# Stick-breaking attention: query blocks of a head in reverse order

## The reference

```python
def stick_breaking_attention(q, k, v):          # 8 heads of 64
    qh = heads(q) * (Dh ** -0.5)
    for blk in range(seq // SB_BLOCK):          # 8 query blocks of 128
        start, end = blk * SB_BLOCK, (blk + 1) * SB_BLOCK
        logits = jnp.einsum('bhtd,bhsd->bhts', qh[:, :, start:end], kh[:, :, :end])
        causal = jnp.arange(end)[None, :] < (start + jnp.arange(SB_BLOCK))[:, None]
        log_remain = jnp.where(causal, jax.nn.log_sigmoid(-logits), 0.0)
        log_after = lax.cumsum(log_remain, axis=3, reverse=True) - log_remain
        weights = jnp.where(causal, jnp.exp(jax.nn.log_sigmoid(logits) + log_after), 0.0)
        outs.append(jnp.einsum('bhts,bhsd->bhtd', weights, vh[:, :, :end]))
```

## Time and profile before

| | us |
|---|---|
| median of 3 runs | 1866.09 (1864.34 to 1867.01) |
| profiled execution | 1864.38, its span 1862.6 |
| TensorE busy, of the span | 1555.1 (83%) |
| VectorE, ScalarE, GpSimd busy | 527.9, 385.5, 265.1 |
| mean granted TensorE clock | 0.924 |
| the mixers stage | 439.7 to 880.1 |
| TensorE in heads 0 to 7, start to start | 54.75, 56.07, 56.51, 55.98, 54.03, 53.01, 56.93, 53.08 |

### The profile page before, as it was taken

One profiled execution on the slowest core, in us unless ns is written; L12 is line 12 of the kernel. 1 busy time (PEld: TensorE's weight loads), 2 busy tenths in 40 slices (PEclk: granted clock), 3 DMA queues, 4 the chain that ended last, 5 costly groups with the idle time before them and its releaser, 6 DMA issues. The chain is left out here.

```text
span 1862.6 us, 19239 instructions
## 1 busy us (share of the span) xinstructions
PE 1555.1 (83%) x6818; PEld 872.1 (47%) x6818; DVE 527.9 (28%) x678; ACT 385.5 (21%) x682; POOL 265.1 (14%) x386
## 2 busy tenths in 40 slices
PE   7999999996989988898389937777778777866997
PEld 4558644444777777776144533232223232323443
DVE  4220133202444444444223241111111111112323
ACT  2221221112343343333021100000000001022221
POOL 1000002101222222221112011111111111110110
PEclk9999999998999999999699958898899898987999
DMA  5220246303110111100711125999999999972220
GB/s 173 72 68 30 81 143 144 96 11 77 29 29 0 28 28 28 28 0 19 304 68 74 39 102 195 419 397 401 399 401 398 402 395 395 408 295 110 94 89 34
DMA packets 93347, 302.95 MB, mean 163 GB/s; under 512 B 13808, under 2 KB 48000, under 8 KB 67328
## 3 DMA queue, kind: packets, MB, share of 16 engines
q1 hardware_dynamic: 83808, 285.69, 41.0%
q0 software_dynamic: 9504, 16.80, 2.4%
HBM read 281.42 MB, written 38.85 MB: 172 GB/s over the span
## 5 line engine op out<-in xcount | busy, mean ns | idle before, releaser
L1381 PE MATMUL pe_gu<-w_gu,xT 128*64 128x512 f32 x1024 | 272.6, 694 | 107.7 <-DMA w_gu<-in_w_expert_up 104.2
L209 PE MATMUL ps<-hT,w_ct 128*128 128x512 f32 x640 | 278.6, 596 | 3.4 <-DVE hT L347 3.4
L1381 PEld LDWEIGHTS pe_gu<-w_gu,xT 128*64 128x64 f32 x1024 | 83.7, 158 | 274.7 <-issue 273.0
L209 PEld LDWEIGHTS ps<-hT,w_ct 128*128 128x128 f32 x640 | 121.4, 191 | 152.7 <-issue 151.2
L724 DVE TENSOR_TENSOR_SCAN Pm<-rem,Pm 128x128 f32<-128x128 f32 (+3 forms) x96 | 97.5, 1016 | 178.2 <-ACT brk L665 178.2
L799 POOL TENSOR_TENSOR wt<-brk,Pm 128x128 f32<-128x128 f32 (+3 forms) x96 | 83.0, 864 | 340.1 <-DVE Pm L724 340.1
L1049 PE MATMUL p_x<-w_o,mT 128*128 128x512 f32 x256 | 121.4, 630 | 2.4 <-DVE mx L1004 1.3
L1474 DVE TENSOR_TENSOR hs<-sg,pe_gu 128x256 f32<-128x256 f32 x32 | 13.5, 421 | 379.9 <-ACT sg L1445 379.9
L1399 PE MATMUL pe_y<-w_d,hTe 128*64 128x512 f32 x512 | 115.5, 592 | 1.1 <-DVE ys L1479 1.1
L1702 PE MATMUL f_pg<-w_gu,f_xT 128*128 128x512 f32 x256 | 114.7, 602 | 1.1 <-ACT f_xT L1620 1.1
L223 PE MATMUL psk<-w_tok,hT 128*128 128x260 f32 (+1 forms) x384 | 111.7, 453 | 0.0
(11 more groups left out here) (266 smaller groups left out, 1738.7 us busy)
## 6 DMA issues: line engine op xcount, KB each, us to landing
w_gu<-in_w_expert_gate SPq DMA_DIRECT2D x64, 1024.0 KB, 13.7
w_gu<-in_w_expert_up SPq DMA_DIRECT2D x64, 1024.0 KB, 15.8
w_d<-in_w_expert_down SPq DMA_DIRECT2D x64, 1024.0 KB, 8.9
w_ct<-in_w_in SPq DMA_DIRECT2D x20, 512.0 KB, 4.4
y_sb<-y_d SPq DMA_DIRECT2D x8, 1024.0 KB, 5.3
qkv_d<-y_sb SPq DMA_DIRECT2D x12, 512.0 KB, 2.7
row_b<-rows_d SPq DMA_DIRECT2D x8, 768.0 KB, 6.7
gst<-qkv_d SPq DMA_DIRECT2D x8, 768.0 KB, 6.4
```

The costliest lines, as they stand in the source:

```text
L209: last = pe.matmul(ps[s][:, c], w_ct[:, s, k, :], hT[:, k, c], start=k == 0, stop=k == KT - 1)
L1381: last = pe.matmul(p_gu[e * CAP:(e + 1) * CAP, :], xT[:, s, k, e * CAP:(e + 1) * CAP], wv[:, e, :, k, :], start=k == 0, stop=k == KT - 1)
```

## The change

The list of strips is built over the query blocks from the last to the first. Within a query block the right strip still comes before the left one. In blocks of 128 keys (m: with the mask of the diagonal):

| step | 0 | 1 | 2 | 3 | 4 | 5 | 6 | 7 | 8 | 9 | 10 | 11 |
|---|---|---|---|---|---|---|---|---|---|---|---|---|
| before | 1m | 2m | 3m | 4m | 1m | 4 | 2m | 4 | 3m | 4 | 4m | 4 |
| after | 4m | 4 | 3m | 4 | 2m | 4 | 1m | 4 | 4m | 3m | 2m | 1m |

```diff
-STRIPS = [(t, c0, min(c0 + 512, (t + 1) * P)) for t in range(NT) for c0 in ((512, 0) if t >= 4 else (0,))]
+STRIPS = [(t, c0, min(c0 + 512, (t + 1) * P)) for t in reversed(range(NT)) for c0 in ((512, 0) if t >= 4 else (0,))]
```

## The result

The changed kernel takes 1882.34 us (median of four runs, 1881.85 to 1885.19), the kernel before 1866.55 beside it: a ratio of 1.0088, 95% interval 1.0071 to 1.0106. The forecast was 1878 with a range of 1864 to 1890. Of the 20.8 us between the two, more than the 15.8 between the medians, 20.4 lie in the mixers stage, which takes 460.7 us from its first logits to its last value product instead of 440.4. The front ended 2.9 us later and the stages behind the mixers took 2.4 us less; no instruction differs there, and nothing is built on either.

What follows compares the result with a forecast made beforehand. A head's length was taken as TensorE's work plus its waits plus clock falls. Moved work and waits, +4.5 us, and clock falls, +7.3, gave +12 on 1864.4, 1876.3; with the runs' median 1.7 higher, 1878, range 1864 to 1890.

Steps and rivals of the forecast that it cites:

- start to kt: Head start to the transposes of k: the wide first strip delays them, +1.64 us in odd heads, +1.48 in even.
- start to y1: Head start to the first product LT times X: +2.88 us, 1.31 of it work brought forward, the rest wait.
- y1 to y2: Delta rule's first to second y product: added strip work fills the wait of 0.92 us, so the interval changes by 0.
- y5 to y6: Between these delta rule products: less TensorE work and a wait down from 0.72 to about 0.2 us, together -1.0.
- y6 to vn: From y6 to the product with R: narrower logits and fewer transposes, -0.89 us; the 1.39 us wait stays.
- The moved work and the waits: All intervals of the eight heads summed, clock aside: +4.5 us, between +2 and +7.
- The table load: ScalarE's load at the top of heads 2, 4 and 6: 1.28 us without a drain; a drain would make +4.5 +9.
- The clock: Longer wait ahead of y1 makes six to seven heads fall to the lower clock instead of four: +7.3 us.
- that the clock stays as it is: Rival for the heads' clock: only the waits move, four heads fall as before: 1871 us, chance 0.20.
- that dense strips cure it: Rival: wide strips behind y1 remove the fall in three or four heads: 1860 us, chance 0.09.
- the even heads didn't fall twice: Rival: the long wait ahead of kt in heads 2, 4, 6 brings its own fall: 1891 us, chance 0.15.
- "drain wins" rival: Narrow strips end each head and front scans hide better, y1 at 9.2 us: 1866 us, chance 0.08.

Runs made afterwards that it cites:

- the run with the wait filled: Changed kernel with the third strip's logits product done three times into the same bank, filling TensorE's wait ahead of y1: 1859.66 us, ratio 0.998.
- moving GpSimd away: Changed kernel with GpSimd's weights of strip 1 waiting until VectorE's copy of XT is done: 1873.82 us, ratio 1.0059.
- the fillings: Third strip's logits product repeated to fill the wait ahead of y1: changed kernel, two added, 1859.66 us; kernel before, one added, 1851.40 us.
- the reversed order with the identities first: Changed kernel, scans of strips 0 and 1 later on VectorE, GpSimd's identity block ahead of strip 0's weights: 1841.24 us, ratio 0.989.

## Why the prediction was right, point by point

Intervals of a head in us, forecast and measured in head 3 (the even heads' row in head 4); y1 to y2 by the run with the wait filled, where the clock is unbroken:

| | before | forecast | after |
|---|---|---|---|
| start to kt, odd heads | 2.76 | 4.4 | 4.37 |
| start to kt, even heads | 3.72 | 5.2 | 5.17 |
| start to y1 | 6.99 | 9.87 | 10.33 |
| y1 to y2, full clock | 6.10 | 6.10 | 6.10 |
| y2 to y3 | 6.65 | 7.1 | 7.07 |
| y3 to y5 | 12.44 | 12.6 | 12.56 |
| y5 to y6 | 6.93 | 5.9 | 6.14 |
| y6 to vn | 7.97 | 7.1 | 7.02 |
| vn to ods | 2.27 | 1.93 | 1.93 |
| ods to the next head | 3.67 | 3.04 | 3.02 |

- *The moved work and the waits*: forecast +4.5 us. The heads at full clock say 54.15 (odd) and 54.85 (even) in the run with the wait filled, against 53.03 and 54.01 in the other: 4 x 1.12 + 4 x 0.84 = +7.8; the medians of the two runs say 1859.66 - 1851.40 = +8.3. The profiled execution of the first still has a fall (head 6, 3.6 us), so that the two figures are this close is in part chance. Each interval but one is within 0.25 us. The term that was mis-sized is the start to y1: 2.88 forecast, 3.34 measured, 8 x 0.46 = 3.7 us. Its cause is shown by moving GpSimd away: y1 then comes at 9.79, and 9.87 was forecast. XT's copy had been priced from a row in which GpSimd's product beside it was two blocks wide.
- *The table load*: its 1.28 us and no drain behind it held (head 2: load at 559.50, sigmoid at 560.80); the odd and even heads differ by 0.80 us ahead of kt, as worked out.
- *The clock*: forecast 2.5 more heads with a fall, +7.3 us. Measured in the profiled pair: all eight, one of them short, so 3.5 more in full falls. From y1 to y2 the eight heads are 24.0 us above 8 x 6.10 in the changed kernel and 11.3 before, +12.7; with the +7.8 that is the stage's 20.4. The medians leave less, 15.8 - 7.8 = 8.0, and so do the fillings, each against the kernel before beside it: 20.0 us for the changed kernel and 12.5 for the kernel before, +7.5, with a fall left in the filled changed kernel. The term lies between 7.5 and 12.7 and can't be told closer: the mean granted clock of single executions of the kernel before goes from 0.922 to 0.928.
- *The rivals*: that the clock stays as it is, and that dense strips cure it, are excluded by the eight rows; the even heads didn't fall twice. The "drain wins" rival fell by y1's row.
- *Luck in it*: the mechanism was right and both sizes came out low, the waits by 3.3 us (7.8 against 4.5) and the clock by 0.2 to 5.4. The number of falls was a guess between bounds (six to seven), since no row showed what a 1.6 us wait does; that the wait became 2.22 and not 1.6 pushed both terms the same way. That 1878 came within 4 us is in part luck.

## What to carry to other kernels

Before reordering strips of different widths among fixed pieces, write down for each engine what stands behind the widest strip in its queue, and in front of which link of the serial chain; the sum of the work doesn't change, the wait of the busiest engine does. A wait of one to two microseconds on TensorE, as this kernel had it, can cost more than its own length again by the clock; test that by giving TensorE a product to throw away there, and if it pays, take the wait itself away. When the wait is for VectorE, look at both of its partners: the scan ahead of it and the GpSimd instruction that runs beside it.

## What the runs showed of the hardware

- With a wait of 1.07 us ahead of y1 four of eight heads fell to the lower clock there, with 1.6 six, with 1.69 and more all, with 0.93 and less none. The wait of 1.39 ahead of vn was followed by none in the kernel before and in the changed one, but not never: the row of 697.30 above shows one, and in four heads (1 and 3 of the changed kernel without GpSimd beside XT's copy, 4 and 7 of the reversed order with the identities first) the lower clock set in 1.9 to 2.1 us behind it. A fall cost 2.5 to 3.3 us of time where the granted clock was 0.50 for 6.8 us, 1.3 to 1.7 where it was for 3.4, and 3.6 in head 6 of the filled changed kernel, where it was for 10.2.
- Two of VectorE's instructions, both with two SBUF inputs, ended late when a GpSimd product had begun before them. XT's copy is 1.24 us beside it and 0.72 without. Sg (St times col_last), which nobody waits for, shows the same by chance: 1.13 us before, when a full strip's product ran beside it (head 3, the first two rows), and 0.68 now that the strip is narrow and its product over, in all eight heads:

```profile
653.82 1.09 POOL L799 TENSOR_TENSOR wt<-brk,Pm 128x512 f32<-128x512 f32 x1 [4.85 <-DVE Pm L724]
654.33 1.13 DVE L760 TENSOR_TENSOR Sg<-St,col_last 128x512 f32<-128x512 f32 x1
```
```profile
L760 DVE TENSOR_TENSOR Sg<-St,col_last x8: 1126/1128/1133, 485.8 to 871.3; 128x512 f32<-128x512 f32 x8
```
```profile
L760 DVE TENSOR_TENSOR Sg<-St,col_last x8: 674/676/678, 493.8 to 896.1; 128x512 f32<-128x512 f32 x8
```

  (in the two last, count, then shortest, median and longest in ns; before, then after). The Trainium skill, page SBUF — State Buffer, section SBUF: two separate sides, says this: the two engines share a port pair, and a VectorE instruction with two SBUF inputs and a GpSimd instruction that reads SBUF exclude each other for a whole instruction. The traces agree: XT's copy and Sg end 0.58 and 0.55 us behind the product, and X's copy, with one input in PSUM, is not held up (0.70). The prediction didn't use this rule. By an estimate from the rows, with XT's copy ending 0.7 us behind a full strip's product, the start to y1 would have come out near 10.4; 10.33 was measured.
